# Norm sums, last weight chunk and opening re-ordered in a two-block transformer kernel

## The reference

```python
def rms_norm_2(x, g):
    xf = x.astype(jnp.float32)
    y = xf * lax.rsqrt(jnp.mean(xf * xf, axis=-1, keepdims=True) + NORM_EPS)
    return (y * g.astype(jnp.float32)).astype(x.dtype)

# second_block, for each layer l:
#   hn = rms_norm_2(h, mix_norm_g[l]);  h = h + mixer(hn)      (even_mixer, then odd_mixer)
#   h = h + conv_ffn(rms_norm_2(h, ffn_norm_g[l]), ffn_w_up[l], ..., ffn_w_down[l])
# return rms_norm_2(h, final_norm_g)
```

## Time and profile before

| | |
|---|---|
| time, median of 3 runs (lowest, highest) | 1646.15 us (1644.98, 1648.76) |
| the profiled execution's own time | 1644.16 us |
| its span, first instruction to last | 1642.4 us |
| TensorE matmuls, busy | 1566.7 us, 95% of the span |
| TensorE weight loads, busy | 1411.5 us, 86% |
| VectorE, busy | 1033.1 us, 63% |
| ScalarE, busy | 748.1 us, 46% |
| GpSimd, busy | 104.5 us, 6% |
| read from memory | 256.41 MB, 157 GB/s over the span |

### The profile page before, as it was taken

How to read it: one execution, slowest core, us unless ns; L and a number is a source line. 1 busy time by engine, 2 the same in 40 slices (tenths; PEclk the granted TensorE clock), 3 DMA queues, 4 the chain that set the end, 5 groups by cost and what they waited for, 6 DMA issues and landing times.

```text
span 1642.4 us, 27303 instructions
## 1 busy us (share of the span) xinstructions
PE 1566.7 (95%) x11312; PEld 1411.5 (86%) x11312; DVE 1033.1 (63%) x1505; ACT 748.1 (46%) x1066; POOL 104.5 (6%) x105
## 2 busy tenths in 40 slices
PE   4998999999999998989999999999999997999997
PEld 3797686887878786968999989999999997999997
DVE  4744756343343347576665668658786878887785
ACT  4213634222232333164544455666564657565553
POOL 0100000000000000000000010201020100020110
PEclk9999999999999998999999999999999999999999
DMA  9752154243242332325445543235455443545551
GB/s 396 285 233 73 68 214 177 105 147 134 102 153 102 133 148 99 107 77 206 156 169 187 187 172 104 94 130 187 180 180 180 166 169 129 180 180 180 181 183 47
DMA packets 36237, 258.81 MB, mean 158 GB/s; under 512 B 4055, under 2 KB 4056, under 8 KB 5168
## 3 DMA queue, kind: packets, MB, share of 16 engines
q1 hardware_dynamic: 29664, 211.85, 35.8%
q0 software_dynamic: 6480, 45.63, 7.3%
HBM read 256.41 MB, written 1.05 MB: 157 GB/s over the span
## 4 chain that ended last, share of the span: by engine, by line
PE 80%; DVE 12%; ACT 5%; issue 2%; DMA 0%; DVEq 0%; SPq 0%; ACTq 0%
PE ps L486 17%; PE ps L488 16%; PE ps L487 16%; PE ps L506 5%; PE ps L507 5%; PE ps L508 5%; PE ps L559 2%; DVE w_lo L1533 2%; PE ps L561 2%; PE ps L560 2%; PE ps L575 2%; ACT w_hi L1083 1%; DVE small L1662 1%; PE ps L598 1%; DVE wgt L1679 1%
## 5 line engine op out<-in xcount | busy, mean ns | idle before, releaser
L1083 ACT ACTIVATE w_hi<-w_raw 128x1024 fp32r<-128x1024 f32 x380 | 397.6, 1056 | 560.0 <-PE ps L488 337.6
L1533 DVE TENSOR_TENSOR w_lo<-w_raw,w_hi 128x1024 fp32r<-128x1024 f32 x380 | 466.3, 1231 | 233.7 <-ACT w_hi L1083 230.3
L486 PE MATMUL ps<-h_hi,w_hi 128*128 128x256 f32 (+1 forms) x1616 | 501.3, 310 | 6.1 <-DVE h_lo L1585 4.5
L487 PE MATMUL ps<-h_lo,w_hi 128*128 128x256 f32 (+1 forms) x1616 | 496.3, 307 | 0.0
L488 PE MATMUL ps<-h_hi,w_lo 128*128 128x256 f32 (+1 forms) x1616 | 496.2, 307 | 0.0
L486 PEld LDWEIGHTS ps<-h_hi,w_hi 128*128 128x128 f32 x1616 | 310.0, 192 | 29.7 <-issue 11.3
L488 PEld LDWEIGHTS ps<-h_hi,w_lo 128*128 128x128 f32 x1616 | 310.1, 192 | 14.1
L487 PEld LDWEIGHTS ps<-h_lo,w_hi 128*128 128x128 f32 x1616 | 310.2, 192 | 13.2
L486 PE MATMUL ps<-g_hi,w_hi 128*128 128x256 f32 (+1 forms) x448 | 140.4, 313 | 0.0
L506 PE MATMUL ps<-g_hi,w_hi 128*128 128x256 f32 (+1 forms) x448 | 140.4, 313 | 0.0
L507 PE MATMUL ps<-g_lo,w_hi 128*128 128x256 f32 (+1 forms) x448 | 140.4, 313 | 0.0
(11 more groups left out here) (327 smaller groups left out, 2225.9 us busy)
## 6 DMA issues: line engine op xcount, KB each, us to landing
w_raw<-in_w_stream SPq DMA_DIRECT2D x190, 1024.0 KB, 4.8
ada_r<-in_w_ada POOLq DMA_DIRECT2D x20, 1024.0 KB, 5.5
ada_g<-in_w_ada POOLq DMA_DIRECT2D x16, 1024.0 KB, 7.5
ada_r<-in_w_ada SPq DMA_DIRECT2D x4, 1024.0 KB, 15.2
ada_g<-in_w_ada SPq DMA_DIRECT2D x4, 1024.0 KB, 25.1
ada_s<-in_w_ada POOLq DMA_DIRECT2D x4, 1024.0 KB, 5.1
x<-in_x_in SPq DMA_DIRECT2D x2, 1024.0 KB, 6.2
pmat<-in_pool_mats POOLq DMA_DIRECT2D x2, 1024.0 KB, 8.0
```

The lines of the kernel that those rows point to most:

```text
L486: mm(o, wh, hi[:, k, cols], start=(k == 0), stop=False)
L487: mm(o, wh, lo[:, k, cols], start=False, stop=False)
L1083: A(w_hi[:, n % 2, k, :].rearrange("p k n -> p (k n)"), w_raw[:, n % 4, k.start * CH:k.stop * CH], ACT.Copy)\
L1533: TT(w_lo[:, n % 2, k, :].rearrange("p k n -> p (k n)"), w_raw[:, n % 4, k.start * CH:k.stop * CH], w_hi[:, n % 2, k, :].rearrange("p k n ...
```

## The change

It has four parts. (1) The last chunk is done m tile by m tile (`last_chunk`); each tile is added, and squared, when it is ready; the four sums of the finished part run while ScalarE squares the last tile; ten matmuls on old data stand before the spread (`last_norm`). ScalarE writes `x` times the gain into `y_out` ahead of the factor (`scaled_out`), and VectorE multiplies two tiles per instruction by the spread factor. `y_out` moves to another place in memory, and the root's table is loaded at the start of the last chunk. (2) In norms 5, 6 and 7 the sums stand before k tile 6 instead of 4, and the spread stands in the next chunk before k tile 2, instead of before k tile 7 of the same chunk. (3) In the opening, ScalarE squares all four pairs of tiles before the SiLU; VectorE adds them before it touches `vec`, copies a row right when its two `w_ada` chunks are done, and TensorE's chunks of `w_ada` and its column matmuls are dealt out between the tiles. (4) TensorE starts with 21 fp32 matmuls of zeros (`diag`, cleared by POOL), and does three more before `w_ada` chunk 2.

```diff
-        y_out = place("y_out", [P, KT, SEQ], at=g_base)
+        y_out = place("y_out", [P, KT, SEQ], at=r_base + 16 * KB)
@@ POOL
             pool.memset(sm(S_EPS), EPS).then_inc(eps_set, 1)
+            pool.memset(diag[:, :, :], 0.0).then_inc(diag_zero, 1)
@@ TensorE, gemm_f
-                        if middle is not None:
-                            middle()
-                    if k == KT - 1 and late is not None:
-                        late()
+                    if k in at_tile:
+                        at_tile[k]()
@@ TensorE, opening
-            def first_group(group):
-                first_ada(2 * group)
-                first_ada(2 * group + 1)
-                first_columns(group)
+            def first_tile(k, n):
+                pe.wait_ge(h_ready, k + 1)
...
+            def keep_busy(count, bank):
+                for _ in range(count):
+                    mm(ps[:, bank, 0:CH], diag[:, 0, :], diag[:, 0:2, :], start=True, stop=True)
+
+            pe.wait_ge(diag_zero, 1)
+            keep_busy(21, 6)
             pe.wait_ge(cst_in_s, 16)
             norm_sums(0)
...
             first_columns(0)
+            keep_busy(3, 4)
+            first_ada(2)
             pe.wait_ge(lam_exp, 1)
-            for k in range(KT):
-                pe.wait_ge(h_ready, k + 1)
-                for n in range(2):
...
-                if k in (0, 1, 3):
-                    first_group((1, 2, None, 3)[k])
+            first_tile(0, 0)
+            first_tile(0, 1)
+            first_ada(3)
+            first_tile(1, 0)
+            first_columns(1)
+            first_tile(1, 1)
+            first_ada(4)
+            first_ada(5)
+            first_tile(2, 0)
+            first_columns(2)
+            first_tile(2, 1)
+            first_tile(3, 0)
+            first_tile(3, 1)
+            first_ada(6)
+            first_ada(7)
+            first_tile(4, 0)
+            first_columns(3)
+            first_tile(4, 1)
+            for k in (5, 6, 7):
+                first_tile(k, 0)
+                first_tile(k, 1)
@@ TensorE, ffn (the same for norm 6 with N_OD)
-                            gemm_f(n, h_hi, h_lo, slice(0, SEQ), (h_ready, H0[f"ffn{l}"]), **norm_inside(5 + 2 * l))
+                            gemm_f(n, h_hi, h_lo, slice(0, SEQ), (h_ready, H0[f"ffn{l}"]),
+                                   at_tile={6: lambda: norm_sums(5 + 2 * l)})
+                        elif c == 1 and third == 0:
+                            gemm_f(n, h_hi, h_lo, slice(0, SEQ), None, at_tile={2: lambda: norm_broadcast(5 + 2 * l)})
@@ TensorE, end
+            def last_chunk(n):
+                start_chunk(n, same)
+                pe.wait_ge(lo_ready, n + 1)
+                s = n % 2
+                for m in range(2):
+                    for k in range(KT):
...
+                    last.then_inc(last_tile, 1)
+            def last_norm():
+                pe.wait_ge(sq_used, 27)
+                for i, part in enumerate((acc2[:, 0], sq[:, 1, 0], sq[:, 1, 1])):
+                    if i:
+                        pe.wait_ge(sums_8, i)
+                    for j in range(2):
+                        last = mm(ps[:, 4 + 2 * j, 0:1], part[:, j * P:(j + 1) * P], ones[:, 0:1], start=(i == 0), stop=(i == 2))
+                last.then_inc(ss_done, 1)
+                for _ in range(10):
+                    mm(ps[:, 0, 0:SEQ], w_hi[:, 0, 0, 0:P], h_hi[:, 0, 0:SEQ], start=True, stop=True)
+                norm_broadcast(8)
@@ ScalarE, opening
-            for j in range(2):
-                act.wait_ge(x_in_s[0], 16)
+            for j in range(4):
+                act.wait_ge(x_in_s[j // 2], 16)
                 squares(0, j)
...
-            for j in (2, 3):
-                act.wait_ge(x_in_s[1], 16)
-                squares(0, j)
             norm_root(0)
@@ ScalarE, end
+            def scaled_out(t):
+                A(y_out[:, t, :], x[:, t, 0:SEQ], ACT.Copy, scale=V("final_g", t)).then_inc(xg_done, 1)
...
+                        if ends and n == N_CHUNKS - 1:
+                            A(sm(S_SQRT), sm(S_EPS), ACT.Sqrt)
+                            act.wait_ge(sq_used, 25)
+                            for m in range(2):
+                                act.wait_ge(last_x, m + 1)
+                                A(sq[:, 1, m, 0:SEQ], x[:, 6 + m, 0:SEQ], ACT.Square).then_inc(sums_8, 1)
+                                if m == 0:
+                                    scaled_out(6)
@@ VectorE, end
-                    for t in range(KT):
-                        STT(y_out[:, t, 0:w], x[:, t, 0:w], V(p1, t), ps[:, 5, 0:w], ALU.mult, ALU.mult).then_inc(out_ready, 1)
+                    for t in range(0, KT, 2):
+                        dve.wait_ge(xg_done, t + 2)
+                        TT(y_out[:, t:t + 2, :], y_out[:, t:t + 2, :], bc(ps[:, 5, 0:w], 2), ALU.mult).then_inc(out_ready, 2)
...
+                        if n == N_CHUNKS - 1:
+                            for m in range(2):
+                                dve.wait_ge(last_tile, m + 1)
+                                TT(x[:, 6 + m, 0:SEQ], ps[:, 2 * (n % 2) + m, 0:SEQ], x[:, 6 + m, 0:SEQ], ALU.add).then_inc(last_x, 1)
+                                if m == 0:
+                                    add_squares(8, 2)
+                            continue
@@ VectorE, opening: the two products on vec stand behind the adds of the squares
+            def first_row(group):
                 dve.wait_ge(ada_done, 2 * group + 2)
                 CP(rows[:, :], ps[:, 7, 0:CH]).then_inc(first_rows, 1)
...
+            first_row(0)
             first_columns(0)
...
             first_lo(1)
+            first_row(1)
+            split_lo(0, parts=(1,))
             for group in range(1, 4):
                 first_columns(group)
                 first_raw(2 * group)
-                if group == 1:
-                    split_lo(0, parts=(1,))
                 first_raw(2 * group + 1)
                 first_lo(2 * group)
                 first_lo(2 * group + 1)
+                if group < 3:
+                    first_row(group + 1)
```

70 lines of the change are left out of this document (42 added, 28 removed).

## The result

The changed kernel takes 1634.45 us, the median of 6 runs (1630.36 to 1639.54), beside 1645.57 for the kernel before on the same chip. The ratio to it is 0.993 (interval 0.991 to 0.995), which makes 11.7 us. Six more runs later gave 1636.51 (1630.21 to 1641.38), ratio 0.994 (0.992 to 0.996), which makes 9.7 us. The forecast was 1636.9, a gain of 9.25 us. The profiled execution took 1638.31 us with a span of 1636.2, so it is one of the slower of these twelve, while the profiled execution of the kernel before (1644.16) is one of the faster of its own; its span is 6.2 us shorter than before. How that fits with 10 to 12 us is part of the answer.

What follows compares the result with a forecast made beforehand. TensorE, busy 95% of the span, bounds the kernel. Gains 4.3 + 1.1 + 0.45 + 0.85 + 2.55 = 9.25 us take the span from 1642.4 to 1633.2, execution 1634.9, median 2.0 above: 1636.9, range 1633 to 1641.5.

Steps and rivals of the forecast that it cites:

- The opening, 4.3 forecast: Start of the program: the opening ends at 56.3 us instead of 60.6, 4.3 us gained, bounds 1.7 and 7.1.
- 1.8 for the clock: Opening: 1.8 us lost to low clock after TensorE stands still for 4 us before `w_ada` 2, bounds 0 and 3.4.
- Idle time: Opening, after 23.55 us: TensorE's waits, such as for rows' copies, taken as 1.0 us instead of 3.06, bounds 0 and 1.96.
- 5.8 us of work to rise: Opening: TensorE starts at low pace and reaches full clock after 5.8 us of work, as read from the earlier trace.
- Costs nothing: Opening: the 21 matmuls of zeros delay nothing while they end before about 15.5 us; 13.4 expected.
- Norms 5 and 7, 1.1 + 0.45 forecast: Sums two k tiles later remove TensorE's stops there: 1.1 us gained at norm 5, 0.45 at norm 7.
- Norm 6, 0.85 forecast: At norm 6 the spread's copy and first scaling (L2185) come earlier, 0.85 us gained, upper bound 2.6.
- the forecast's lower bound (0.65): Norm 6: if the clock falls there again, the spread comes 1.5 us later and 0.65 us is lost.
- mostly swallowed: Norm 6: TensorE's own 1.1 us and the low clock's 1.5 us mostly don't count, as ScalarE and VectorE set the pace.
- The end, 2.55 forecast: After the last weight matmul: root 1.3 us earlier, spread 0.55 and scalings 0.7 shorter, together 2.55 us gained.
- 1.7 us each either way: Later in the program: stretches of low clock fall elsewhere when everything shifts, worth 1.7 us each, widening the range.
- a rival's sum, 30.6 + 29.9 + 3.4: Opening, zeros do not raise the clock: it ends near 64.1 us, 3.5 later; total 1644.7, no change; chance 0.06.

Runs made afterwards that it cites:

- the experiment on the opening: Kernel before with parts 3 and 4 of the change alone: 1640.69 us, ratio 0.9971.
- the experiment on the norms: Kernel before with part 2 alone (sums of norms 5, 6 and 7 before k tile 6, spread in the next chunk): 1643.03 us, ratio 0.9984.
- the experiment on the end alone: Kernel before with part 1 alone (last chunk tile by tile, new last norm): 1643.64 us, ratio 0.9983.

## Why the prediction was right

**The opening, 4.3 forecast.** The first profile shows 6.5, the experiment on the opening 3.7 in its profile and 4.8 in its runs. The difference lies in one thing that changes from execution to execution. In five profiles of this opening with lead-in and three zeros the stop is 3.57 to 3.60 us each time; behind it `w_ada` 2 took 1.07 once and 1.93 or 1.94 four times, and the opening ended at 53.79, 54.99, 56.09, 56.57 and 56.64, on average 55.6. The forecast, counted to the same start, was 56.0. The term "1.8 for the clock" was thus no constant: it was 0 once and otherwise cost 1.2 to 2.9, with `w_ada` 2's own half pace, which I had left out. Idle time was forecast 1.0 and is 0.42, as only the wait for the row of tiles 4 and 5 is left. That the two errors nearly cancel is luck. The first tile started at 24.50 or at 25.2 to 25.5, forecast 24.6. That the clock takes 5.8 us of work to rise was no constant either: in the experiment on the norms, whose opening is that of before, the `w_ada` chunk at 20.14 still took 1.93, and the opening ended at 60.87 instead of 60.32.

**The lead-in.** It ended between 12.07 and 13.58 (12.28 in the first profile), forecast 13.4, and the sums ran at full pace, so matmuls of zeros do raise the clock. "Costs nothing" was right for the sums and wrong for the whole: the 2.9 to 3.5 us that it saved ahead of the transfer became the stop of 3.6 us behind which the clock can fall. Without it the stop is 0 to 0.64 us with the three zeros in place. I had forecast the stop and put a price on it, but had not charged it to the lead-in. The zeros as a whole (part 4) bought nothing that can be seen: the one profile without any ends its opening at 55.35, the average with all of them is 55.6. By these profiles the new order (part 3) alone accounts for the gain.

**Norms 5 and 7, 1.1 + 0.45 forecast.** The idle rows are gone, and from the sums of norm 5 to those of norm 6, where both lie 1.44 us later in the program, 208.66 us are left of 209.86: 1.2, the size of norm 6's stop, which was as long as norm 5's (0.96 in both rows). At norm 7 the profile of the norms alone has 204.54 us from the sums to the last chunk's add and the kernel before 206.06; with the 1.44 by which the sums moved and the stop of 0.48, that is 0.56 gained. No `w_lo` is waited for behind norms 5 and 7.

**Norm 6, 0.85 forecast.** Counted from where k tile 4 was reached: before 0.96 + 0.16 + 6.08 = 7.20 to `od_s`, now 1.44 + 4.82 = 6.26, so 0.94. But 1.5 of the 7.20 was the low clock behind the sums. In the experiment on the end alone it stayed away at this norm, and before's order needed 1.12 + 4.54 = 5.66: at full clock the changed order is 0.6 slower. That is about the size of the forecast's lower bound (0.65), but not its case, which was a fall in the new order; none was seen. The 0.85 rested on the clock staying up in the new order, for which the forecast gave no reason, while it called the 1.5 "mostly swallowed"; the gain at this norm is just that fall that stays away. The three falls in six cases with the stop, against none in 22 without it, suggest that this is the work of the order, as the stop is gone, and that norm 5 profits as well; it is a comparison of few profiles, and no experiment was made for it. Over both norms together it comes out the same each time: from k tile 4 at norm 5 to k tile 4 at norm 7 the three profiles with the order of before took 310.1 to 310.4 us, the first profile of the changed kernel 307.9, so 2.2 to 2.5 less, 1.95 forecast. The order that wins in both cases is the spread before k tile 0: 1.44 + 3.42 = 4.86.

**The end, 2.55 forecast.** The root comes 1.45 earlier (forecast 1.3), the step from root to spread is 0.13 longer (forecast unchanged), the spread 0.63 shorter (0.55 forecast for it), the scalings 0.74 (0.7): 2.6 from the last add's start to the last scaling's end (8.47 us before, 5.84 now). The stores were left out: from the last scaling's end to the span's end there are 3.0 us, 2.5 before (2.9 to 3.2 in all eleven profiles with the new end, 2.5 in all three with the old). The four stores are issued 0.6 us apart now, 256 KB each, and take 2.5 us from issue to landing instead of 2.0 (medians). That takes back 0.6; what is left is 2.1.

**The sum.** 55.6 for the opening's end gives 4.7, the norms 2.8 to 3.1, the end 2.1: 9.6 to 9.9, forecast 9.25, measured 9.7 and 11.7, each give or take 3 to 4. Of the first profile's 6.2 us, the opening gave 6.5 and what follows the sums of norm 6 another 4.25; in between it took 4.6 us longer than before. The same kernel's second profile takes 9.0 us less for that stretch, and over all eleven profiles with the changed opening the way from its end to the sums of norm 5 takes 1051.6 to 1061.1 us, on average 1055.7 (0.3 of it, in ten of them, from the later place of the sums), against 1053.0 to 1055.3 in the three with the opening of before. So the loss belongs to the low clock of that execution and not to the change. The sentence that low clock moves "1.7 us each either way" was right for one stretch and too small for their number: single executions of the changed kernel differ by up to 11 us. In a rival's sum, 30.6 + 29.9 + 3.4 is 63.9 and not 64.1, which changes nothing.

The Trainium skill (TensorE: Matmul & The Clock Gate, HAM oscillation) describes a kernel whose matmuls wait some 3 to 5 us for each transfer and come back at the low clock each time. The runs agree in most cases and not in all: low behind stops of 3.57, 3.58, 3.59, 3.60 and 4.78 us, high behind one of 3.59. The stop of 1.72, also low, and that of 0.64, high, are shorter than the waits that the page describes. The stop at 25.81, with which the prediction compared, was a wait for VectorE and not for a transfer.

**The best version.** No lead-in, three zeros, norm 6's spread before k tile 0: median 1631.62, ratio 0.9917, against 1634.45 and 1636.51 of the changed kernel. The profiles explain 2.6 us: the opening ends at 54.1 here and at 54.7 in the other kernel with the same opening, 1.2 before the average of 55.6, and norm 6 gives 1.4. The kernel without the lead-in alone has the same median, 1631.65, so the runs don't show what the early spread adds. The intervals of its ratio and of the changed kernel's overlap, so that it beats the changed kernel is likely and not shown; that it beats the kernel before is.

## What to carry to other kernels

Before work ahead of a fixed transfer is made faster, or an engine is warmed up, ask where the freed time goes: if into the wait for that transfer, little is gained and the clock may be lost; fill the stop or leave the work slow. A short stop ahead of very short matmuls is worth removing for more than its own length, if the clock tends to fall behind it. A term that depends on the granted clock is a distribution: take a second profile of the same kernel before a difference of a few microseconds between two profiles is given to a cause. And where several engines set the pace behind a spread factor, move the factor itself forward, not only the stop in front of it away.
